# Stacked keys, split sums and fourteen moved pieces in a one-core transformer kernel

## The chip, the core and the metric

The kernel runs on one core of a Trainium2 chip. Its time is the device time of one execution in microseconds (us). The engines work at the same time and meet at semaphores: TensorE (PE; its weight loads are listed apart, as PEld), VectorE (DVE), ScalarE (ACT), GpSimd (POOL) and SyncE (SP), whose queue issues DMA transfers.

## The reference, cut to what matters

Six mixer layers and two feed-forward layers run over 512 tokens of width 1024: pooling, convolution, latent attention, pooling, and then two attention layers (l = 0, 1), each with a feed-forward layer. The attention layers compute eight heads of stick-breaking attention (dimension 64) and four of differential attention.

```python
z = jnp.einsum('bhqd,bhkd->bhqk', qblk, kh).astype(jnp.float32) * scale
strict = kpos[None, :] < qp[:, None]
log_beta = jax.nn.log_sigmoid(z)
log_keep = jnp.where(strict, jax.nn.log_sigmoid(-z), 0.0)
between = lax.cumsum(log_keep, axis=log_keep.ndim - 1, reverse=True) - log_keep
w = jnp.where(strict, jnp.exp(log_beta + between), 0.0)
```

Each layer begins with an RMS norm, `xf * rsqrt(mean(xf * xf) + eps) * g`, which needs the sum of squares over the 1024 features of each token.

## The kernel before

**Numbers.** Activations lie with features on the 128 partitions and tokens along the row. A float32 matrix is held as two tiles of the type fp32r, a high part and what is left (low). A product is then three matmuls, high x high, high x low, low x high (`mm3`, lines 414 to 416). ScalarE makes the high part (`high`, L941), VectorE the low part (`low`, L1556). Weights come by DMA into four `raw` tiles, 512 KB each; ScalarE copies them to `wh` (L932), VectorE (L1548) or GpSimd (L2327) makes `wl`. A weight unit of 128 columns in eight blocks is `gemm8`: 24 matmuls of 512 columns.

**Order.** Every engine has a program of its own, written out by hand, in `pe_program`, `act_program`, `dve_program`, `pool_program` and `sp_program`; each instruction waits for the results that it names and runs in its place. In an attention layer the order is a list of calls in `second_layer(l)` of each program. PSUM has eight banks. Three are kept for the stick-breaking scores (`sb_banks`), the others are taken in the order of `LAYER_BANKS`; a bank is waited for until its reader has marked it free.

**Sums of squares.** ScalarE squares, GpSimd adds up into `ACC`, and `sum_squares` (L442) multiplies by a matrix of ones in full float32, which the profile shows as two records. A use is a norm: 0 to 3 are the first four layers, "kv" and "q" the latent norms, 4 and 6 open the attention layers, 5 and 7 the feed-forward layers, ("df", l, h) the differential heads. ScalarE's `root` (L963) and VectorE's `recip_root` (L1564) turn the sum into the factor `R`, which the results of the projections are multiplied by afterwards; so the projections run ahead of it, and `gemm8(norm=...)` puts the sum inside a projection. The convolution layer calls `sum_squares(1)` between its first two projections (`cc`, `ch`; `cb` and `cz` follow).

**Stick-breaking scores.** `proj("sq", p)` and `proj("sk", p)` make queries and keys of two heads, 64 partitions each. VectorE scales them, `plain` splits them. `sb_scores(h)` multiplies for each of four key blocks (`GR`: 256 + 128, 384 and 512 columns in three banks) 64 rows of keys with 64 rows of queries, and adds a mask with 128-row products of `identr` and `hidden` (L752). Then follow `soft` (softplus; ACT, DVE), `keep` (split), `sb_between` (running sums on TensorE, L766 and L767), `weights_of` (exponential and split) and `sb_pv` (product with the values). `df_scores(h, base)` (L787 to L792) works on 64-row products of both halves of the partitions, `df_turn` transposes (L544), `df_pv` and `df_squares` follow, and `wo(half, m, parts)` is the output projection. `rot` splits a rotated query or key of the differential heads after GpSimd has added its parts (L2350).

Of the kernel before, what the change touches and what calls it, by code (L numbers as in the profile page):

```python
# [15 lines left out]
S = 512  # L16
# [20 lines left out]
for _name, _n in (("pool_norm0", 8), ("pool_norm1", 8), ("pool_scale0", 16), ("pool_scale1", 16),  # L37
# [26 lines left out]
LAYER_BANKS = (  # L64
# [3 lines left out]
LAST_BANKS = (0, 6, 5, 1, 3, 7, 2, 4)  # L68
LAST_ROWS = (1, 0, 4, 2, 3, 5, 7, 6)

SEMS = ("xin0", "xin1", "xin2", "xin3", "xin4", "xin5", "xin6", "xin7", "consts", "vec", "raw0", "raw1", "raw2", "raw3", "pos", "lam", "cos", "sin", "fn", "out",
        "group", "whi", "wlo", "wlop", "act", "dve", "pool")
# [25 lines left out]
class Counts:  # L98
# [7 lines left out]
    def mark(self, name, *results, by=1):  # L106
        self.total[name] += by
        for r in results:
            assert r not in self.value or r[0] in ("accfree", "wfree", "stored"), r
            self.value[r] = (name, self.total[name])  # L110
        return self.sems[name], by
# [176 lines left out]
def program(nc, D, out):  # L288
    ctx = ExitStack()
    with ctx:  # L290
# [66 lines left out]
        def sqk(p):  # L357
            return (YH[2], YL[2], YH[3], YL[3]) if p == 1 else G[8:12]
# [22 lines left out]
        def linit(l):  # L381
            return 0.8 - 0.6 * math.exp(-0.3 * l)

# [8 lines left out]
        def pe_program(handle, c):  # L392
# [25 lines left out]
            def gemm8(key, h, l, ready=None, norm=None):  # L418
# [277 lines left out]
            def second_layer(l):  # L696
# [38 lines left out]
                def sb_scores(h):  # L735
                    p, e = h // 2, h % 2
                    q_h, q_l, k_h, k_l = sqk(p)
                    rr = slice(64 * e, 64 * e + 64)
                    pe.wait_ge(*at("pl", l, "sq", p))
                    pe.wait_ge(*at("pl", l, "sk", p))  # L740
                    pe.wait_ge(*at("ones"))
                    for n, (kbs, k0, width) in enumerate(GR):
                        b = use(sb_banks[n], ("ss", l, h, kbs[0]))
                        for kb in kbs:
                            o = b[:, KOFF[kb] - k0:KOFF[kb] - k0 + 512 - 128 * kb]
                            kc, qc = slice(kb * 128, kb * 128 + 128), slice(kb * 128, 512)
                            mm3(o, k_h[rr, kc], k_l[rr, kc], q_h[rr, qc], q_l[rr, qc], kb == kbs[0], False)
                    for kbs, k0, width in GR:
                        b = ps("ss", l, h, kbs[0])
                        for kb in kbs:  # L750
                            o = b[:, KOFF[kb] - k0:KOFF[kb] - k0 + 128]
                            mm = pe.do.matmul(o, identr[:, :], hidden[:, :], start=False, stop=kb == kbs[-1])  # L752
                        mm.then_inc(*mark("group", ("mm", "ss", l, h, kbs[0])))
# [71 lines left out]
                v_part(0, 0, 0), norms(), v_part(0, 0, 1), proj("sq", 0), proj("sk", 0), v_part(0, 1, 0)  # L825
                sb_scores(0), proj("dq", 0), v_part(0, 1, 1), proj("dk", 0)
                sb_between(0), proj("sq", 1), sb_scores(1), df_scores(0, 34), sb_pv(0), proj("dk", 1)
                proj("sk", 1)
                sb_between(1), df_scores(0, 32), df_scores(0, 16), proj("dk", 2), proj("dq", 1), sb_scores(2)
                v_part(1, 1, 0), df_turn(0), v_part(1, 1, 1), sb_pv(1), v_part(1, 0, 0), df_scores(1, 34)  # L830
                v_part(1, 0, 1)
                sb_between(2), sb_scores(3), df_pv(0), df_scores(1, 32), df_scores(1, 16), proj("dq", 2)
                df_squares(0), proj("dq", 3), sb_pv(2), proj("sk", 2), proj("sq", 2), df_scores(2, 34)
                df_turn(1)
                sb_between(3), df_pv(1), df_scores(2, 32), sb_scores(4), df_scores(2, 16), proj("dk", 3)
                df_squares(1), sb_pv(3), proj("sq", 3), df_turn(2)
                sb_between(4), df_pv(2), df_scores(3, 34), sb_scores(5), df_scores(3, 32), wo(0, 2), wo(0, 0)
                sb_pv(4), proj("sk", 3), df_scores(3, 16)
                sb_between(5), wo(0, 1), df_squares(2), sb_scores(6), wo(0, 4), df_turn(3), sb_pv(5), df_pv(3)
                wo(0, 5), wo(0, 3)  # L840
                sb_between(6), wo(0, 6), sb_scores(7), sb_pv(6), df_squares(3), wo(1, 2, (0, 1))
                wo(1, 1, (0, 1)), wo(0, 7), wo(1, 0, (0, 1))
                sb_between(7), wo(1, 1, (2,)), wo(1, 4, (0, 1, 2)), wo(1, 3, (0, 1, 2)), sb_pv(7)
                wo(1, 0, (2,)), wo(1, 2, (2,)), wo(1, 1, (3,)), wo(1, 0, (3,)), wo(1, 4, (3,)), wo(1, 2, (3,))
                wo(1, 3, (3,)), wo(1, 5), wo(1, 7), wo(1, 6)
# [67 lines left out]
        def act_program(handle, c):  # L913
# [312 lines left out]
            def second_layer(l, done):  # L1226
# [27 lines left out]
                def plain(nm, p):  # L1254
                    dst = sqk(p)[0 if nm == "sq" else 2]
                    if p > 1:
                        act.wait_ge(*at("mm", "ss", l, 2 * p - 3 if p == 2 else 5, 0))
                    high(dst[:, :], temp("pj", l, nm, p), ("pj", l, nm, p), ("plh", l, nm, p))
# [97 lines left out]
                soft(0)  # L1356
                keep(0)
# [6 lines left out]
                weights_of(0)  # L1364
                taking('sq', l, 1)
                rot("dk", 0)
                taking('dk', l, 1)
# [1368 lines left out]
```

## Time and profile before

| | |
|---|---|
| median of 3 runs | 2719.13 us (2718.26 to 2719.65) |
| the profiled execution | 2719.73 us |
| its span, first to last instruction | 2717.9 us |
| TensorE busy | 99% of the span |
| VectorE, ScalarE, GpSimd busy | 58%, 42%, 23% |
| TensorE's share of the chain that ended last | 93% |
| mean granted clock of TensorE | 0.998 |

Times in the rows are in us from the start of the span. A matmul's record runs from its start until its results have landed, and records overlap; how fast matmuls follow each other is read from start to start. `128x512` is partitions x columns. A view's brackets give the idle time of the engine before an instruction, and who ended it.

### The profile page before, as it was taken

How to read it: one execution, taken by the hardware profiler on the slowest of the kernel's cores; microseconds unless marked ns; L12 is line 12 of the kernel's file. 1: busy time of each engine (PE TensorE's matmuls, PEld its weight loads, DVE VectorE, ACT ScalarE, POOL GpSimd, SP SyncE). 2: the span in 40 equal slices, each digit the busy share in tenths (PEclk: the TensorE clock that was granted, in tenths of full speed). 3: DMA queues.
4: the chain of work that ended last, by engine and by line, in shares of the span. 5: the costliest groups of instructions: out<-in, count | busy, mean ns of one | idle time of the engine just before them, and what ended most of it. 6: DMA issues, size and time to landing. Idle time of an engine off the chain costs nothing.

```text
span 2717.9 us, 31965 instructions
## 1 busy us (share of the span) xinstructions
PE 2694.4 (99%) x12918; PEld 2254.4 (83%) x12918; DVE 1576.7 (58%) x2307; ACT 1150.4 (42%) x1831; POOL 625.6 (23%) x401
## 2 busy tenths in 40 slices
PE   8999999999999999999999999999999999999999
PEld 7888888888888888888888888788888888788887
DVE  7556545344466646665575678744445668754444
ACT  4323323222347636533235767422224667522223
POOL 1000111011136525400004642411102452411100
PEclk9999999999999999999999999999999999999999
DMA  4232332332221222222322221233333221233332
GB/s 162 95 99 93 99 100 93 101 101 93 90 80 56 72 69 67 93 95 99 96 98 88 80 68 33 85 94 101 93 101 102 72 63 47 70 97 97 94 99 79
DMA packets 69412, 238.78 MB, mean 88 GB/s; under 512 B 7696, under 2 KB 10256, under 8 KB 69264
## 3 DMA queue, kind: packets, MB, share of 16 engines
q1 hardware_dynamic: 69264, 236.73, 27.6%
q8 instruction: 102, 1.67, 0.3%
q14 instruction: 46, 0.38, 0.0%
HBM read 234.60 MB, written 2.10 MB: 87 GB/s over the span
## 4 chain that ended last, share of the span: by engine, by line
PE 93%; DVE 3%; ACT 2%; POOL 1%; issue 0%; DMA 0%; SPq 0%; ACTq 0%; POOLq 0%
PE ps L414 30%; PE ps L416 29%; PE ps L415 29%; DVE ptl L1556 1%; PE ps L544 1%; PE ps L442 1%; ACT wh L932 0%; PE ps L767 0%; PE ps L766 0%; POOL acc L2336 0%; PE ps L604 0%; PE ps L605 0%; ACT pth L941 0%; DMA raw<-in_pool_in 0%; PE ps L466 0%
## 5 line engine op out<-in xcount | busy, mean ns | idle before, releaser
L932 ACT ACTIVATE wh<-raw 128x1024 fp32r<-128x1024 f32 (+2 forms) x453 | 465.0, 1028 | 741.7 <-PE ps L416 738.5
L414 PE MATMUL ps<-xh,wh 128*128 128x512 f32 x1920 | 753.5, 392 | 0.0
L416 PE MATMUL ps<-xh,wl 128*128 128x512 f32 x1920 | 747.5, 389 | 0.0
L415 PE MATMUL ps<-xl,wh 128*128 128x512 f32 x1920 | 747.3, 389 | 0.0
L1548 DVE TENSOR_TENSOR wl<-raw,wh 128x1024 fp32r<-128x1024 f32 (+1 forms) x339 | 449.4, 1326 | 151.2 <-ACT wh L932 151.0
L414 PE MATMUL ps<-yh,wh 128*128 128x512 f32 x1088 | 425.1, 391 | 2.6 <-ACT t L960 1.6
L414 PEld LDWEIGHTS ps<-xh,wh 128*128 128x128 f32 x1920 | 360.5, 188 | 76.4 <-issue 2.2
L415 PEld LDWEIGHTS ps<-xl,wh 128*128 128x128 f32 x1920 | 360.5, 188 | 76.0 <-issue 2.2
L415 PE MATMUL ps<-yl,wh 128*128 128x512 f32 x1088 | 423.5, 389 | 0.0
L416 PE MATMUL ps<-yh,wl 128*128 128x512 f32 x1088 | 423.4, 389 | 0.0
L416 PEld LDWEIGHTS ps<-xh,wl 128*128 128x128 f32 x1920 | 360.3, 188 | 75.2
L2327 POOL TENSOR_TENSOR wl<-raw,wh 128x1024 fp32r<-128x1024 f32 (+2 forms) x114 | 255.4, 2249 | 378.1 <-ACT wh L932 378.0
L1582 DVE TENSOR_TENSOR x<-ps,x 128x512 f32<-128x512 f32 x152 | 104.3, 689 | 265.2 <-PE ps L416 265.2
L2336 POOL TENSOR_TENSOR acc<-acc,t 128x512 f32<-128x512 f32 x59 | 84.1, 1425 | 721.2 <-ACT t L953 719.2
L414 PEld LDWEIGHTS ps<-yh,wh 128*128 128x128 f32 x1088 | 204.2, 188 | 48.2 <-issue 4.3
L416 PEld LDWEIGHTS ps<-yh,wl 128*128 128x128 f32 x1088 | 204.2, 188 | 42.6
L415 PEld LDWEIGHTS ps<-yl,wh 128*128 128x128 f32 x1088 | 204.3, 188 | 41.7
L2521 POOL TENSOR_TENSOR t<-t 128x512 f32<-128x512 f32 x64 | 71.2, 1116 | 513.4 <-DVE t L2256 513.4
L941 ACT ACTIVATE yh<-t 128x512 fp32r<-128x512 f32 x148 | 93.1, 631 | 169.4 <-POOL t L2521 56.7
L1556 DVE TENSOR_TENSOR yl<-t,yh 128x512 fp32r<-128x512 f32 x148 | 114.6, 775 | 82.7 <-ACT yh L941 82.7
L1560 DVE SCALAR_TENSOR_TENSOR xl<-x,vec,xh 128x512 fp32r<-128x512 f32 x64 | 83.1, 1315 | 60.3 <-ACT xh L943 60.3
L2256 DVE SCALAR_TENSOR_TENSOR t<-ps,r 128x512 f32<-128x512 f32 x64 | 44.1, 689 | 104.3 <-PE ps L416 104.0
(261 smaller groups left out, 3647.7 us busy)
## 6 DMA issues: line engine op xcount, KB each, us to landing
raw<-in_ff SPq DMA_DIRECT2D x120, 512.0 KB, 3.6
raw<-in_pool_in SPq DMA_DIRECT2D x64, 512.0 KB, 3.3
raw<-in_conv_in SPq DMA_DIRECT2D x64, 512.0 KB, 3.3
raw<-in_pool_out SPq DMA_DIRECT2D x32, 512.0 KB, 3.3
raw<-in_qk SPq DMA_DIRECT2D x32, 512.0 KB, 3.7
raw<-in_pool_grp SPq DMA_DIRECT2D x16, 512.0 KB, 3.3
raw<-in_conv_out SPq DMA_DIRECT2D x16, 512.0 KB, 3.3
raw<-in_mla_z SPq DMA_DIRECT2D x16, 512.0 KB, 3.6
```

The source lines that it names most:

```text
L414: pe.do.matmul(o, lh, rh_, start=start, stop=False)
L415: pe.do.matmul(o, lh, rl_, start=False, stop=False)
L416: return pe.do.matmul(o, ll, rh_, start=False, stop=stop)
L932: act.do.activation(h[:, 0:ncol], r[:, 0:ncol], ACT.Copy).then_inc(*mark("whi", ("whi", k)))
L941: act.do.activation(dst, src, ACT.Copy).then_inc(*mark("act", done))
L1548: dve.do.tensor_tensor(lo[:, 0:ncol], r[:, 0:ncol], f(h[:, 0:ncol]), ALU.subtract).then_inc(*mark("wlo", ("wlo", k)))
L1556: dve.do.tensor_tensor(dst, src, f(h), ALU.subtract).then_inc(*mark("dve", *done))
L1560: dve.do.scalar_tensor_tensor(dst, src, scale, f(h), ALU.mult, ALU.subtract).then_inc(*mark("dve", *done))
L1582: dve.do.tensor_tensor(x[m][:, :], ps(*key)[:, :], x[m][:, :], ALU.add).then_inc(*mark("dve", ("psfree",) + key, *done))
L2327: pool.do.tensor_tensor(lo[:, 0:ncol], r[:, 0:ncol], f(h[:, 0:ncol]), ALU.subtract).then_inc(*mark("wlop", ("wlo", k)))
L2336: pool.do.tensor_tensor(ACC[:, :], ACC[:, :], temp("sq", use, k), ALU.add).then_inc(*mark("pool", ("acc", use, k), ("tfree", "sq", use, k)))
L2521: pool.do.tensor_tensor(t, t, t, ALU.mult).then_inc(*mark("pool", ("ffs",) + key))
```

## The change

Stacked keys: a key tile of a pair of heads becomes two tiles. Tile e holds the high part of head e's keys on that head's partitions, and the low part on the other 64. The high part of the query is put on both halves of the partitions by DMA copies inside the chip, issued by ScalarE (two for the even head, one, `double`, for the odd). One 128-row matmul then gives high x high and low x high, a 64-row matmul the third product. The mask of the two joined blocks is one matmul. Split sums: for uses 1, 2, 3, 5 and 7 `ACC` is split into high and low, and the sum is two fp32r matmuls; the place of the sum inside the projection changes for all uses that `gemm8` places. The rest are moves within the programs; new bank lists go with them.

```diff
-LAYER_BANKS = (
+LAYER_BANKS = (
...
+SUMS_SPLIT = (1, 2, 3, 5, 7)
+NORM_AT = 5
...
         def sqk(p):
-            return (YH[2], YL[2], YH[3], YL[3]) if p == 1 else G[8:12]
+            q0, ql_, k0, k1 = (YH[2], YL[2], YH[3], YL[3]) if p == 1 else G[8:12]
+            return (q0, (YL[1], YH[1], YH[2], YH[3])[p]), ql_, (k0, k1)
...
+        def sum_parts(use):
+            return (PTH[:, 0:S], PTL[:, 0:S]) if use == 2 else (DFH[:, 0:S], DFL[:, 0:S])
...
-                    if norm is not None and k == 2:
+                    if norm is not None and k == (NORM_AT if norm in SUMS_SPLIT else 4):
                         sum_squares(norm)
...
+                if use in SUMS_SPLIT:
+                    pe.wait_ge(*at("ones"))
+                    pe.wait_ge(*at("suml", use))
+                    h, lo = sum_parts(use)
+                    pe.do.matmul(b[:, :], onesr[:, :], h, start=True, stop=False)
+                    pe.do.matmul(b[:, :], onesr[:, :], lo, start=False, stop=True).then_inc(
+                        *mark("group", ("mm", "rs", use)))
+                    return
...
-                              norm=st if g == 0 and i == (1 if j else 3) else None)
+                              norm=st if g == 0 and i == 3 else None)
...
                         xgemm(1, "cc", i, first=i == 0)
-                        if i == 0:
-                            sum_squares(1)
-                        xgemm(1, "ch", i)
+                        xgemm(1, "ch", i, norm=1 if i == 0 else None)
...
-                    pe.wait_ge(*at("pl", l, "sk", p))
+                    pe.wait_ge(*at("plx", l, p) if e == 0 else at("pl", l, "sk", p))
+                    pe.wait_ge(*at("dup", l, p, e))
...
-                            mm3(o, k_h[rr, kc], k_l[rr, kc], q_h[rr, qc], q_l[rr, qc], kb == kbs[0], False)
+                            pe.do.matmul(o, ks[e][:, kc], qs[e][:, qc], start=kb == kbs[0], stop=False)
+                            pe.do.matmul(o, ks[e][rr, kc], q_l[rr, qc], start=False, stop=False)
...
+                        o, cover = b[:, 0:128], hidden[:, :]
+                        if len(kbs) == 2:
+                            o = b[:, 0:512].rearrange("p (a c) -> p a c", a=2)[:, :, 0:128]
+                            cover = hidden[:, :].rearrange("p (a c) -> p a c", a=1).to_broadcast([128, 2, 128])
+                        pe.do.matmul(o, identr[:, :], cover, start=False, stop=True).then_inc(
+                            *mark("group", ("mm", "ss", l, h, kbs[0])))
...
 def root (ACT):
+                if use in SUMS_SPLIT:
+                    high(sum_parts(use)[0], ACC[:, :], last_square(use), ("sumh", use))
...
 def recip_root (DVE):
+                if use in SUMS_SPLIT:
+                    h, lo = sum_parts(use)
+                    low(lo, ACC[:, :], h, ("sumh", use), ("suml", use), ("accfree", use))
...
 def plain (ACT):
+                    if nm == "sk":
+                        high(ks[0][0:64, :], t[0:64, :], ("pj", l, nm, p), ("plhx", l, p))
+                        high(ks[1][64:128, :], t[64:128, :], ("pj", l, nm, p), ("plh", l, nm, p))
+                        return
...
+                    high(qs[1][:, :], t, ("pj", l, nm, p), ("plh", l, nm, p))
+                    act.wait_ge(*at("plh", l, nm, p))
+                    for rr in (slice(0, 64), slice(64, 128)):
+                        act.do.dma_start(f(qs[0][rr, :]), f(qs[1][0:64, :])).then_inc(*mark("dupa", ("dup", l, p, 0), by=16))
+
+                def double(p):
+                    q = sqk(p)[0][1]
+                    act.wait_ge(*at("dup", l, p, 0))
+                    act.wait_ge(*at("pl", l, "sq", p))
+                    if l or p:
+                        act.wait_ge(*at("dup", l, p - 1, 1) if p else at("dup", l - 1, 3, 1))
+                    act.do.dma_start(f(q[0:64, :]), f(q[64:128, :])).then_inc(*mark("dupb", ("dup", l, p, 1), by=16))
...
 def plain (DVE):
+                    if nm == "sk":
+                        low(ks[0][64:128, :], t[0:64, :], ks[0][0:64, :], ("plhx", l, k), ("plx", l, k))
+                        low(ks[1][0:64, :], t[64:128, :], ks[1][64:128, :], ("plh", l, nm, k), ("pl", l, nm, k),
```

`double(0)` and `double(1)` stand on ScalarE behind `soft(0)` and `keep(1)`, `double(2)` and `double(3)` behind `df_exp(2, 34)` and `df_exp(3, 16)`.

The moves, per engine. TensorE: `df_scores(0, 32)` ahead of `sb_between(1)`; `sb_scores(3)` from before `df_pv(0)` to behind `df_scores(1, 16)`; `df_scores(3, 32)` from behind `sb_scores(5)` to before `df_scores(3, 34)`; `df_turn(3)` ahead of `wo(0, 4)`; `wo(1, 3)` ahead of `wo(1, 4)`. ScalarE: `weights_of(0)` from before `taking("sq", 1)` to behind `rot("dk", 0)`; `x_high(st + 1, 1)` behind `x_high(st + 1, 2)`. VectorE: `df_join(0)` and `turned("dk", 2)` behind `rot("dk", 1)` and `turned("dq", 1)`; `v_low(1, 0)` ahead of `between(2)`; `df_max(2, 34)` ahead of `df_turn(1)`; `sb_out(3)` ahead of `between(4)`. GpSimd: the first two value units change places, and `scale_x(7)` with `taking("v", 0, 1, 1)` comes before `scale_x(5)`.

## Rows read from the trace of the kernel before

**Rows 1.** The page: its span and the busy time of each engine.

```profile
span 2717.9 us, 31965 instructions
...
PE 2694.4 (99%) x12918; PEld 2254.4 (83%) x12918; DVE 1576.7 (58%) x2307; ACT 1150.4 (42%) x1831; POOL 625.6 (23%) x401
...
```

**Rows 2.** Timeline, TensorE, head 0: start us, duration us, engine, line, operation.

```profile
...
1495.09 0.28 PE L416 MATMUL ps<-wh,xl 128*128 128x256 f32 x1
...
1495.52 0.28 PE L415 MATMUL ps<-g 64*128 64x256 f32 x1
1495.64 0.28 PE L416 MATMUL ps<-g 64*128 64x256 f32 x1
...
1496.27 0.33 PE L415 MATMUL ps<-g 64*128 64x384 f32 x1
1496.44 0.33 PE L416 MATMUL ps<-g 64*128 64x384 f32 x1
...
1496.85 0.39 PE L415 MATMUL ps<-g 64*128 64x512 f32 x1
1497.08 0.39 PE L416 MATMUL ps<-g 64*128 64x512 f32 x1
...
```

**Rows 3.** Timeline, TensorE's weight loads, the same head.

```profile
...
1495.30 0.18 PEld L414 LDWEIGHTS ps<-g 64*128 64x128 f32 x1
...
1497.40 0.52 PEld L752 LDWEIGHTS ps<-hidden,identr 128*128 128x128 f32 x4 [0.37 <-issue]
1497.84 0.19 PEld L414 LDWEIGHTS ps<-xh,wh 128*128 128x128 f32 x1
...
```

**Rows 4.** Waits of TensorE, first attention layer: total us, times, longest us.

```profile
...
PE ps L414 <- ACT t L960: 0.8, 1, 0.8
...
```

**Rows 5.** DMA issues: KB each, median us from issue to landing.

```profile
...
t<-in_lam SPq DMA_DIRECT2D x2, 128.0 KB, 2.0
...
```

**Rows 6.** Timeline, TensorE, the sum of squares of use 1.

```profile
...
322.00 1.02 PE L442 MATMUL ps<-acc,const 128*128 128x512 f32 x2
...
323.09 0.40 PE L415 MATMUL ps<-xl,wh 128*128 128x512 f32 x1
...
```

**Rows 7.** Timeline, TensorE, the sum of squares of use 0.

```profile
...
27.48 0.39 PE L416 MATMUL ps<-xh,wl 128*128 128x512 f32 x1
28.59 1.12 PE L442 MATMUL ps<-acc,const 128*128 128x512 f32 x2 [0.72 <-POOL acc L2336]
...
```

**Rows 8.** Timeline, VectorE and TensorE, start of the convolution layer.

```profile
...
325.11 3.35 DVE L1564 RECIPROCAL r<-t 128x512 f32<-128x512 f32 x1 [3.94 <-ACT t L963]
...
329.90 1.22 DVE L1548 TENSOR_TENSOR wl<-raw,wh 128x1024 fp32r<-128x1024 f32 x1
...
333.78 0.39 PE L414 MATMUL ps<-xh,wh 128*128 128x512 f32 x1
...
```

**Rows 9.** Timeline, all engines, around the first differential scores.

```profile
...
1517.59 0.53 ACT L1297 ACTIVATE s<-s 128x384 f32<-128x384 f32 x1 [0.33 <-PE ps L767]
...
1518.96 1.53 POOL L2350 TENSOR_TENSOR t<-t 128x512 f32<-128x512 f32 x1 [0.32 <-DVE t L1716]
...
1520.20 0.63 ACT L941 ACTIVATE pth<-s 128x512 fp32r<-128x512 f32 x1
...
1522.33 2.47 DVE L1556 TENSOR_TENSOR yl<-t,yh 128x512 fp32r<-128x512 f32 x1 [0.78 <-ACT yh L941]
...
1525.70 0.50 PE L787 MATMUL ps<-yh 64*128 64x512 f32 x1
...
```

**Rows 10.** Busy time by stretch; PEclk is the mean granted clock.

```profile
...
1690.00:1710.00 20.00, 18.84 (x89) 15.31 (x88) 13.22 (x21) 11.37 (x21) 5.08 (x2) 0.91 0.18 53
1702.00:1704.00 2.00, 2.00 (x7) 1.81 (x7) 1.97 (x5) 0.00 (x0) 0.00 (x0) 0.50 0.46 172
2323.00:2326.00 3.00, 3.00 (x12) 2.71 (x11) 2.55 (x6) 0.00 (x0) 0.00 (x0) 0.50 0.39 137
...
```

**Rows 11.** Timeline, TensorE, the product behind the scores of head 7.

```profile
...
1701.35 0.65 PE L414 MATMUL ps<-pth,g 128*128 128x512 f32 x1 [0.38 <-DVE ptl L1556]
...
```

More of the change, by code:

```diff
@@ L108, in mark @@
         for r in results:
-            assert r not in self.value or r[0] in ("accfree", "wfree", "stored"), r
+            assert r not in self.value or r[0] in ("accfree", "wfree", "stored", "dup"), r
             self.value[r] = (name, self.total[name])
@@ L845, in second_layer @@
-                wo(1, 3, (3,)), wo(1, 5), wo(1, 7), wo(1, 6)
+                v_part(0, 0, 0)
+                norms()
+                v_part(0, 0, 1)
+                proj("sq", 0)
+                proj("sk", 0)
+                v_part(0, 1, 0)
+                sb_scores(0)
+                proj("dq", 0)
+                v_part(0, 1, 1)
+                proj("dk", 0)
+                sb_between(0)
+                proj("sq", 1)
+                sb_scores(1)
+                df_scores(0, 34)
+                sb_pv(0)
@@ new lines, in second_layer @@
+                proj("dk", 1)
+                proj("sk", 1)
+                df_scores(0, 32)
+                sb_between(1)
+                df_scores(0, 16)
+                proj("dk", 2)
+                proj("dq", 1)
+                sb_scores(2)
+                v_part(1, 1, 0)
+                df_turn(0)
+                v_part(1, 1, 1)
+                sb_pv(1)
+                v_part(1, 0, 0)
+                df_scores(1, 34)
+                v_part(1, 0, 1)
+                sb_between(2)
@@ new lines, in second_layer @@
+                df_pv(0)
+                df_scores(1, 32)
+                df_scores(1, 16)
+                sb_scores(3)
+                proj("dq", 2)
+                df_squares(0)
+                proj("dq", 3)
+                sb_pv(2)
+                proj("sk", 2)
+                proj("sq", 2)
+                df_scores(2, 34)
+                df_turn(1)
+                sb_between(3)
+                df_pv(1)
+                df_scores(2, 32)
+                sb_scores(4)
+                df_scores(2, 16)
@@ new lines, in second_layer @@
+                proj("dk", 3)
+                df_squares(1)
+                sb_pv(3)
+                proj("sq", 3)
+                df_turn(2)
+                sb_between(4)
+                df_pv(2)
+                df_scores(3, 32)
+                df_scores(3, 34)
+                sb_scores(5)
+                wo(0, 2)
+                wo(0, 0)
+                sb_pv(4)
+                proj("sk", 3)
+                df_scores(3, 16)
+                sb_between(5)
+                wo(0, 1)
@@ new lines, in second_layer @@
+                df_squares(2)
+                sb_scores(6)
+                df_turn(3)
+                wo(0, 4)
+                sb_pv(5)
+                df_pv(3)
+                wo(0, 5)
+                wo(0, 3)
+                sb_between(6)
+                wo(0, 6)
+                sb_scores(7)
+                sb_pv(6)
+                df_squares(3)
+                wo(1, 2, (0, 1))
+                wo(1, 1, (0, 1))
+                wo(0, 7)
+                wo(1, 0, (0, 1))
+                sb_between(7)
@@ L846, in second_layer @@
+                wo(1, 1, (2,))
+                wo(1, 3, (0, 1, 2))
+                wo(1, 4, (0, 1, 2))
+                sb_pv(7)
+                wo(1, 0, (2,))
+                wo(1, 2, (2,))
+                wo(1, 1, (3,))
+                wo(1, 0, (3,))
+                wo(1, 4, (3,))
+                wo(1, 2, (3,))
+                wo(1, 3, (3,))
+                wo(1, 5)
+                wo(1, 7)
+                wo(1, 6)
                 first_pair(st + 1, [("f1", l, 0, 0), ("f1", l, 0, 1)], LAST_ROWS)
@@ L1464, in second_layer @@
                 taking('wo', l, 1, 1)
-                x_high(st + 1, 1)
                 x_high(st + 1, 0)
@@ L1469, in second_layer @@
                 x_high(st + 1, 2)
+                x_high(st + 1, 1)
                 taking('wo', l, 1, 3)
@@ L2467, in second_layer @@
                 taking('v', l, 0, 1, 0)
+                scale_x(7)
+                taking('v', l, 0, 1, 1)
                 scale_x(5)
```

62 lines of the change are left out of this document (24 added, 38 removed), and 3 rows, old and new, of the table LAYER_BANKS.

## The prediction

> **What bounds the kernel now.** I read the page first: TensorE is busy 2694.4 of 2717.9 us, so in this kernel only TensorE's own instructions and its waits can move the time; the other engines matter where TensorE waits for them [rows 1]. A busy share says little about how fast an instruction gives way to the next, so the second view was TensorE's timeline around one head of the stick-breaking scores, read by the distance from start to start. Three-pass products of 128 rows follow each other every 0.12 us with 256 columns; in the scores, 384 columns take 0.17 (1496.27 to 1496.44) and 512 take 0.23 (1496.85 to 1497.08) [rows 2]. The weight loads beside them show what the matmul rows hide. Four loads in a row, from 1497.40 to 1497.84, are 0.11 us each, so a 128-column product cannot go faster than 0.11. And where the number of active rows changes (128 to 64 at the start of the head, 64 to 128 at its end), the load does not run under the product before it: that product, started at 1495.09, has streamed by 1495.21, and the load starts at 1495.30; the one started at 1497.08 has streamed by 1497.31, and the load starts at 1497.40 [rows 2, 3]. Idle 0.09 plus a bare load of 0.11: a change of row count costs about 0.20 us. By the starts of the products it is 0.19 (1495.09 to 1495.52 is 0.43, for two products of 0.12). Third view: who TensorE waits for. In the first attention layer it has seven lines, the longest single wait 0.8 [rows 4]. So a layer is bound by TensorE, and the vector and scalar engines are just behind it in a few places.
>
> **Part 1, stacked keys.** Per head the score product of each of four key blocks goes from three matmuls to two: one of 128 rows (high and low keys stacked over a doubled query), one of 64 rows (high keys, low query). Saved: one each of 256, 128, 384 and 512 columns, 0.12 + 0.11 + 0.17 + 0.23 = 0.63 us [rows 2, 3]. The mask goes from four products of 128 columns to one of 256 and two of 128: 0.44 becomes 0.34, so 0.10 more. But the two kinds now alternate. Before, a head is one run of 64-row products: two changes. Now it is 128, 64, 128, 64, 128, 64, 128, 64 and then the mask (128): eight changes, four runs. Two of the products between changes have 128 columns and need only their 0.06 of streaming (128 columns of the 0.23 for 512), since the load is already in the price of the change: 2 x 0.05 = 0.10 comes off. Savings per head 0.83, for 8 heads and 2 layers 13.3 us.
>
> Runs of 64-row products in a layer, counted along TensorE's program. Before: the eight heads and ten pieces of differential scores, of which two touch a head's run (df 2/32 with head 4, df 3/34 with head 5): 16 runs. After: 8 x 4 = 32 of the heads, and ten of the differential scores (0/32 and 0/16 are torn apart by `sb_between(1)`, 3/32 and 3/34 are joined), none of which can merge, because a head now begins with a 128-row product: 42 runs. That is 26 more runs, 52 more changes a layer, 104 in all, at 0.195: +20.3 us (19.8 to 20.8 by the two readings). **Part 1: 20.3 - 13.3 = +7.0 us.** A head by itself goes from 2.74 us (1495.21 to 1497.95, which is the last load's start plus 0.11) to about 3.08.
>
> The rule for this is in the Trainium skill. "TensorE: Matmul & The Clock Gate", section "Step-by-step: what each phase is for", says that TensorE pulls a weight load ahead of a running matmul when it goes to the background buffer; by that alone the changes would be free and part 1 would be -11.7 us. The loads at 1495.30 and 1497.40 were not pulled ahead [rows 3], so I keep it as a rival only.
>
> **Part 2, what part 1 asks of the others.** Each key tile is split in halves: one more scalar-engine copy and one more vector subtraction per pair. TensorE waits for the first half alone for the even head, so nothing is later for it. The doubled query comes by copies of 128 KB, three per pair, issued by the scalar engine. A load of that size lands 2.0 us after its issue [rows 5]; between the query's projection and the first scores lie a projection (24 x 0.227 = 5.4 us) and a value part (48 x 0.12 = 5.8 us), and for the other pairs more. I count the copies at nothing; uncovered, a copy would cost at most its 2.0 us per pair, 16 us in all, at the least nothing. The same window hides the halves. The issue itself holds the scalar engine; no row shows a copy inside the chip or an issue there, so between 0 and 2.0 us each, near 0 since the engine only hands it over.
>
> **Part 3, split sums.** A sum of squares in full precision takes, from 322.00 to 323.09 less the 0.23 of the product that stands between, 0.86 us [rows 6]. Two single-pass products of 512 columns take 0.45. Five uses: 5 x -0.41 = **-2.0 us**. Use 0 stays as it is but is asked for six products (1.4 us) later. It is due at 27.48 + 0.23 = 27.71 and starts at 28.59, with a bare load of 0.11 [rows 7]: the accumulation is late by 0.9. Two more k-steps cover that: **-1.0**.
>
> Each moved sum makes its root later. In the convolution layer the sum moves from behind the first projection to k = 5 of the second: 15 x 0.227 = 3.4 later, less 0.4 for its two shorter products: 3.0. Behind it hang a table load, the root, the reciprocal of 3.35 us (325.11), and the low part of the fourth projection's weights, which ends at 329.90 + 1.22 = 331.12; TensorE starts that projection at 333.78 [rows 8]. Slack 2.7. After: ready 334.1, wanted 333.78 - 0.41 = 333.37, and a bare load on top: **+0.9 us**. At the other four (3.0 less six products) the root is 1.6 to 2.3 later, and TensorE has two or more projections of 5.4 us before it wants anything from it: nothing.
>
> **Part 4, the pieces that move.** `weights_of(0)` goes behind `rot("dk", 0)` on the scalar engine. That rotation needs the GpSimd sum which ends at 1518.96 + 1.53 = 1520.49. Now the weights' six activations start at 1517.59 and end at 1520.83; after the move they start at 1521.1 and end at 1524.4. The vector engine takes the low parts first and the rotation's after them: 1525.1 plus 0.7 to 2.5 (it took 2.47 at 1522.33, beside GpSimd): 1525.8 to 1527.6. The differential scores 0/34, at 1525.70 now and 0.35 later by head 1, want it at 1526.05 [rows 9]. So 0 to 1.5 us a layer; I take 0.7: **+1.4**. Queued behind it on the scalar engine are `plain("sq", 1)` and the softplus of head 1, for which `sb_between(1)` has 10 us. The mirror of it: two waits are covered by longer heads, the one in front of `sb_pv(6)` (0.35 of its 0.38 [rows 11]) and the first output projection (0.3): 0.65 a layer, **-1.3**. The sum-of-squares wait of 0.8 [rows 4] stays: the same bank is reused right behind it. The waits around 1647 to 1651 hang on the vector engine after head 4 and move along with it. The swaps among the output projections, `x_high(1)`, `scale_x(7)` and the two value units on GpSimd lie more than a projection ahead of their readers: nothing, at worst one subtraction (0.7) each way.
>
> **Part 5, the clock.** The granted clock is 0.50 (1.2 GHz) at 1702 to 1704 and at 2323 to 2326 [rows 10]; before the first, TensorE did the scores of head 7 and waited 0.38 [rows 11]. A mean of 0.91 over 20 us is 0.09 x 20 / 0.5 = 3.6 us at 0.50, of which half, 1.8, is lost each time. The new scores hold more idle time per head than the old. From two such falls to all sixteen heads is 14 x 1.8 = +25, to none -3.6; I take one more, as heads 4 and 6 now stand beside other thin work: **+1.8**. On this "TensorE: Matmul & The Clock Gate" (section "A second HAM failure mode: psum-queue depth-cycling") says that frequent short idles between groups of matmuls make the clock swing; the trace shows it at two places of sixteen.
>
> **Sum.** +7.0 - 2.0 - 1.0 + 0.9 + 1.4 - 1.3 + 1.8 = +6.8 us on the profiled execution's 2719.73, of which 1.8 lie outside its span. The median of the runs shown is 0.6 below it. Forecast 2719.13 + 6.8 = **2725.9 us**, slower by 0.25%. This kernel's runs differ by 0.05%; 0.2% (5.4 us) is what a measurement can tell from no change.
>
> **Rivals.** *A: the changes of row count are free*, since weights load ahead; the place is each head, and it decides as soon as a change costs under 0.13 us (13.3 / 104). Part 1 becomes -11.7; the sum is then -11.7 - 2.0 - 1.0 + 0.9 + 1.4 = -12.4, of which the vector engine's chain gives back 1 or 2 at the waits around 1647: 2708, faster. For it: different rows of the array could be loaded independently. Against it: all the changes in the trace cost 0.19 or more. *B: the clock stays up.* The longer head 7 covers the wait before `sb_pv(6)`, the two falls vanish, and `rot` is in time: 7.0 - 3.0 + 0.9 - 1.3 - 3.6 = 0.0, 2719.1, no change. For it: that wait, of 0.38, stands right before the fall. Against it: the idle time inside the heads grows. *C: the clock falls at most light heads*, say five more times: +9.0 in place of +1.8, 2733. For it: two heads of sixteen do it already.
>
> **Chances.** Forecast 0.45 (its own range 2721 to 2730), A 0.10, B 0.28, C 0.17. Range 2716 to 2735: it leaves out A and the far end of C. Faster by over 0.2% is A: 0.10. Within 0.2%: B and the lower quarter of the forecast, 0.37. Slower: the rest and C, 0.53.
>
> **What would show it.** In the changed profile, weight loads of the scores that start 0.09 after the end of streaming at every change, a head of 3.1 us; sums of 0.45; a wait of 0.9 on the fourth projection's weights near 333; no wait near 28; a wait of up to 1.5 before the first differential scores; granted clock 0.50 in two to four places. Wrong it is if a head takes under 2.7 us (then A), if the differential scores wait for nothing, or if a wait for a copy of the queries appears.

## The result and the profile after

| | before | changed |
|---|---|---|
| median | 2718.26 us (13 runs, 2716.45 to 2719.65) | 2726.14 us (13 runs, 2723.34 to 2738.17) |
| profiled execution | 2719.73 | 2738.17 |
| its time at granted clock 0.50 inside the layers | 6.8 us | 34.1 us |
| the same execution without what that cost (half of it) | 2716.3 | 2721.1 |

The ratio is 1.0037, interval 1.0030 to 1.0044: slower by 7.9 us, forecast 6.8. The profiled execution is one of three of the thirteen in which the clock was low for longer, so the two profiles are compared without the clock: +4.8 us (forecast without its clock term: +5.0). That leaves some 3.1 of the 7.9 to the clock in the median run, and less if the subtraction takes off too much (see the experiments). One execution of the kernel before, of 27 that ran beside e4, e6, e7 and e8, took 13369.91 us and is left out of the ratios.

The page of the changed kernel, against [rows 1]:

```profile
span 2736.4 us, 31864 instructions
...
PE 2708.6 (99%) x12838; PEld 2256.4 (82%) x12838; DVE 1585.1 (58%) x2320; ACT 1158.6 (42%) x1844; POOL 619.8 (23%) x401
```

TensorE issues 80 products fewer and is busy 14 us longer. Timeline of TensorE, head 0, against [rows 2]:

```profile
1493.51 0.28 PE L757 MATMUL ps<-g 128*128 128x256 f32 x1
1493.72 0.38 PE L758 MATMUL ps<-g 64*128 64x256 f32 x1
...
1495.28 0.50 PE L757 MATMUL ps<-g 128*128 128x512 f32 x1
1495.71 0.50 PE L758 MATMUL ps<-g 64*128 64x512 f32 x1
1496.14 0.56 PE L765 MATMUL ps<-hidden,identr 128*128 128x256 f32 x3
1496.54 0.45 PE L417 MATMUL ps<-xh,wh 128*128 128x512 f32 x1
```

Its weight loads, against [rows 3]:

```profile
1494.91 0.18 PEld L758 LDWEIGHTS ps<-g 64*128 64x128 f32 x1 [0.19 <-issue]
1495.28 0.19 PEld L757 LDWEIGHTS ps<-g 128*128 128x128 f32 x1 [0.19 <-issue]
1495.71 0.18 PEld L758 LDWEIGHTS ps<-g 64*128 64x128 f32 x1 [0.25 <-issue]
```

Two products of 512 columns are 0.43 apart, not 0.23: at a change of row count each load begins with the product's own record, 0.09 after the one before has streamed, and none is ahead. This head is 3.03 us (1493.51 to 1496.54). Waits of TensorE in the first layer (total, times, longest), against [rows 4]:

```profile
PE ps L800 <- DVE yl L1669: 2.1, 1, 2.1
PE ps L417 <- DVE ptl L1669: 1.9, 2, 1.6
PE ps L553 <- DVE t L2102: 0.8, 1, 0.8
PE ps L417 <- ACT t L1051: 0.8, 1, 0.8
PE ps L779 <- DVE ptl L1669: 0.5, 1, 0.5
```

6.1 us, where before it was 4.0 in seven lines. The wait before `sb_pv(6)` and the one before the first output projections are gone as forecast. New are the 2.1 (before `df_scores(3, 32)`), the 1.6 of the second line (before the value product `df_pv(1)`) and the 0.8 before the transposes of `df_turn(1)`. The granted clock in stretches of the first layer, against [rows 10]:

```profile
1525.00:1528.00 3.00, 3.00 (x11) 1.98 (x8) 2.68 (x5) 1.80 (x5) 1.25 (x1) 0.50 0.50 109
...
1658.00:1668.00 10.00, 9.86 (x28) 6.56 (x29) 7.09 (x17) 6.38 (x14) 0.00 (x0) 0.50 0.13 51
```

A third, of 3.4 us, begins at 1634.05, and the same three places show it in the second layer. Before them stand head 1, head 4, and, at 1658, the new wait of 2.1.

### The profile page after: what moved, and what is told of

It reads as the page before. It is cut to its first block, busy times and chain, and to the rows that moved or that the text cites. A ratio compares the mean times of both kernels' runs of the same rounds, so it can differ in the third digit from the quotient of the medians.

```text
span 2736.4 us, 31864 instructions
## 1 busy us (share of the span) xinstructions
PE 2708.6 (99%) x12838; PEld 2256.4 (82%) x12838; DVE 1585.1 (58%) x2320; ACT 1158.6 (42%) x1844; POOL 619.8 (23%) x401
## 4 chain that ended last, share of the span: by engine, by line
PE 93%; DVE 4%; ACT 2%; issue 1%; ACTq 0%; DMA 0%; SPq 0%; DVEq 0%
PE ps L417 29%; PE ps L419 29%; PE ps L418 29%; DVE ptl L1669 1%; PE ps L758 1%; PE ps L553 1%; PE ps L757 1%; PE ps L779 1%; PE ps L780 1%; DVE yl L1669 1%; PE ps L486 0%; PE ps L613 0%; PE ps L614 0%; ACT t L1157 0%; PE ps L453 0%
## 5 line engine op out<-in xcount | busy, mean ns | idle before, releaser
L1030 ACT ACTIVATE yh<-t 128x512 fp32r<-128x512 f32 (+1 forms) x152 | 95.7, 631 | 181.0 <-POOL t L2641 58.5
```

The costliest lines, as they stand in the source:

```text
L1030: act.do.activation(dst, src, ACT.Copy).then_inc(*mark("act", done))
```

## The experiments

"Against before" is the difference of medians to runs of the kernel before on the same chip (medians 2717.64 to 2718.26). "Clock-free" is the profiled execution less half its time at 0.50. It is an estimate from one execution, and can be off by 2 us or more. The start of the kernel alone moves it: the changed kernel and the seven that differ from it only in the attention layers have the same program up to the convolution's sum of squares, and begin that sum between 324.32 us (e2) and 325.82 (e7). And it takes off too much where TensorE would have waited anyway. Of each execution that was timed without a profile the record has the mean granted clock to three digits, where 0.001 is 2.7 us. In e8 those at 1.000 took 2716.9 to 2717.5 us and one at 0.997 took 2717.65, though half of its time at 0.50 is 6.8 us or more; the column says 2714.9 for e8. Of the changed kernel one took 2726.63 at 0.999 and another 2725.28 at 0.997: without half of their time at 0.50 they are at least 4 us apart. Differences between kernels below are of these two columns.

| kernel | median | against before | ratio, interval | clock-free |
|---|---|---|---|---|
| before | 2718.26 | | | 2716.3 |
| changed | 2726.14 | +7.9 | 1.0037 (1.0030 to 1.0044) | 2721.1 |
| e1 scores grouped | 2714.82 | -2.9 | 0.9991 (0.9982 to 1.0000) | 2713.5 |
| e2 all score products 128 rows | 2713.39 | -4.3 | 0.9984 (0.9975 to 0.9993) | 2713.0 |
| e3 before, masks in between | 2744.00 | +26.3 | 1.0096 (1.0082 to 1.0109) | 2723.6 |
| e4 before, split sums | 2715.37 | -2.3 | 0.9992 (0.9983 to 1.0002) | 2713.3 |
| e5 changed, not stacked | 2719.32 | +1.6 | 1.0008 (0.9999 to 1.0017) | 2712.5 |
| e6 changed, two waits on GpSimd | 2722.54 | +4.9 | 1.0019 (1.0010 to 1.0028) | 2714.5 |
| e7 grouped, two waits | 2708.75 | -8.9 | 0.9966 (0.9953 to 0.9979) | 2709.1 |
| e8 grouped, no moves | 2719.15 | +1.5 | 1.0003 (0.9994 to 1.0012) | 2714.9 |
| e9 grouped, three waits | 2706.97 | -10.9 | 0.9960 (0.9947 to 0.9972) | 2706.7 |
| e10 as e9, one move undone | 2707.18 | -10.7 | 0.9956 (0.9943 to 0.9970) | 2707.4 |

**e3: changes of row count alone.**

```diff
 in the loop over key blocks:
     mm3(o, k_h[rr, kc], k_l[rr, kc], q_h[rr, qc], q_l[rr, qc], kb == kbs[0], False)
+    o = b[:, KOFF[kb] - k0:KOFF[kb] - k0 + 128]
+    mm = pe.do.matmul(o, identr[:, :], hidden[:, :], start=False, stop=kb == kbs[-1])
 (and not in a loop behind it)
```

> The kernel before, with one edit: each mask product (128 rows) stands right behind the three 64-row products of its block and not behind all twelve. Nothing is added or taken away. Changes of row count per head go from 2 to 8, 96 more in all. Theory: 96 x 0.195 = +18.7, less 0.05 for each of three masks per head whose load is in the price of the change (-2.4): +16.3, so 2718.3 becomes 2734.6, and a head grows from 2.6 to 3.6 us. Rival A (changes are free): 2718. A price half as large, if a part is hidden by the next product's streaming: 2726.

Timeline of TensorE, head 2 of e3:

```profile
1559.78 0.38 PE L414 MATMUL ps<-yh 64*128 64x256 f32 x1
...
1560.12 0.27 PE L416 MATMUL ps<-yh,yl 64*128 64x256 f32 x1
1560.33 0.33 PE L749 MATMUL ps<-hidden,identr 128*128 128x128 f32 x1
1560.58 0.32 PE L414 MATMUL ps<-yh 64*128 64x128 f32 x1
...
1563.35 0.50 PE L414 MATMUL ps<-wh,xh 128*128 128x256 f32 x1
```

The head is 3.57 us (1559.78 to 1563.35) against 2.60 for the same sixteen products in the old order: 0.97 for six changes and 0.15 saved, 0.19 a change. Rival A is out. The median rose by 26.3, more than the 16.3 expected, and the clock is why: nine stretches at half clock, 44.4 us, of which this is one (columns as in [rows 10]).

```profile
1598.00:1604.00 6.00, 6.00 (x25) 4.94 (x24) 0.78 (x2) 1.32 (x4) 0.00 (x0) 0.50 0.22 81
```

Clock-free it is +7.3, where sixteen heads have 15.5 more: in the first layer waits fall from 4.0 to 2.3 us, so some 3.4 of it is cover for waits; the other 4.8 no view accounts for, and part of it is what the subtraction takes off too much in nine stretches. Alternating row counts alone brings the clock down here: the edit only reorders, and TensorE's waits are shorter than before.

**e5: the changed kernel without the stacked keys.**

```diff
-pe.do.matmul(o, ks[e][:, kc], qs[e][:, qc], start=kb == kbs[0], stop=False)
-pe.do.matmul(o, ks[e][rr, kc], q_l[rr, qc], start=False, stop=False)
+mm3(o, k_h[rr, kc], k_l[rr, kc], q_h[rr, qc], q_l[rr, qc], kb == kbs[0], False)
 (key tiles, masks and splits as before; no copies)
```

> The changed kernel without the stacked keys: products, masks, key tiles and the absence of copies are those of the kernel before; split sums and all moves stay. The forecast's sum for these is -2.0 - 1.0 + 0.9 + 1.4 - 1.3 = -2.0, or 0 without the cover that the longer heads give: 2716 to 2718, 8 to 10 us under the changed kernel. Rival (the stacked keys cost nothing, the moves do): 2723 to 2726. The profile tells which of the new waits (2.1 before a differential score, 1.6 before a value product) belong to the moves: they stay here if they do.

The stacked keys cost 6.3 us in the median (forecast part 1: 7.0), clock-free 8.6. Waits of its first layer:

```profile
PE ps L795 <- DVE yl L1642: 2.2, 1, 2.2
PE ps L416 <- DVE ptl L1642: 1.3, 2, 0.9
```

The wait of 2.2 is there without the stacked keys; the split sums alone (e4) have 1.3 before the differential scores that stand at that point, the kernel before 0.4, so the moves bring the rest. All waits of this layer are 4.8 us, 1.3 less than in the changed kernel, whose waits before `df_pv(1)` and `df_turn(1)` are longer. The median is above the 2716 to 2718 expected, the clock-free time below them.

**e4: the kernel before with the split sums alone** (the sum's hunks of the diff, no others).

> The kernel before with the split sums alone: uses 1, 2, 3, 5 and 7 as two single-pass products behind five k-steps, use 0 behind four, the convolution's inside its second projection. No stacked keys, no moves. The forecast's terms: -2.0 - 1.0 + 0.9 = -2.1. The trace of the changed kernel shows no wait where the +0.9 was expected (the weights' low part ends at 332.28, the projection starts at 332.85), which would make it -3.0: 2714.7 beside a before of 2717.7. Rival: the sums were hidden by the vector engine's chain in the layers and only the front gains: -2.2. Rival: nothing, 2717.7.

-2.3 in the median, an interval that just reaches no change, and -3.0 clock-free. The executions at a mean clock of 1.000 are clearer: three of e4 took 2714.2 to 2715.3 us, seven of the kernel before, run beside it, 2716.3 to 2717.2. With e5 that gives the moves, without stacked keys: clock-free -0.8, in the median +3.9. The loss is in the clock: the mean is 0.996 to 0.998 in all executions of e5, 0.998 to 1.000 in e4's.

**e1: the 64-row products of a head together.**

```diff
 for each of the four key blocks:
+    pe.do.matmul(o, ks[e][rr, kc], q_l[rr, qc], start=kb == kbs[0], stop=False)
 then for each of them again:
+    pe.do.matmul(o, ks[e][:, kc], qs[e][:, qc], start=False, stop=False)
```

> The changed kernel, with one edit: in each head of the stick-breaking scores the four 64-row products come first, then the four 128-row ones, then the masks. Same products, same columns; only the changes between 64 and 128 active rows are fewer. Counted along TensorE's program a layer has 42 runs of 64-row products now and 15 with the edit (three pieces of differential scores merge with a head): 54 changes fewer a layer, 108 in all. Theory (each change costs 0.195 us): -21.1, and +1.6 for 128-column products that are bound by their load again, so about -19.5: 2726.1 becomes 2706.6, and a head takes 2.7 us in place of 3.03 to 3.12... less in the profile by 0.3 or more; below 2704 if the clock falls less often. Rival A (the changes are free): 2726, same. Rival B (the loss is the vector engine's waits, and faster heads only make them longer): 2715 to 2722, waits of TensorE grow by 4 to 6 us a layer.

Timeline of TensorE, head 0 of e1:

```profile
1493.94 0.90 PE L757 MATMUL ps<-g 64*128 64x256 f32 x4
1494.77 0.90 PE L763 MATMUL ps<-g 128*128 128x256 f32 x4
1495.51 0.46 PE L770 MATMUL ps<-hidden,identr 128*128 128x256 f32 x3
1495.80 0.45 PE L417 MATMUL ps<-xh,wh 128*128 128x512 f32 x1
```

The head falls from 3.03 to 1.86 with 0.09 more ahead of it: 1.08 less, by the price 6 x 0.195 - 0.10 = 1.07 (the head of 2.7 in the expectation was a slip). But of 19.5 us only 10.8 arrive. Clock-free e1 is no faster than e5, which does not stack at all (2713.5 and 2712.5, closer than that column can tell apart). Some of its waits in the first layer, 10.2 us in all (6.1 in the changed kernel, 4.8 in e5):

```profile
PE ps L417 <- ACT ob L1445: 2.3, 2, 1.3
PE ps L417 <- DVE ptl L1674: 2.2, 2, 1.6
PE ps L805 <- DVE yl L1674: 1.7, 2, 1.2
```

TensorE's products in a layer take 5.8 us less than e5's by their distances (0.227, 0.173, 0.12, 0.11), and it waits 5.4 longer for the vector and scalar engines instead. What e1 gains on e5 is clock, by the same column: 6.8 us at 0.50 in place of 13.7, and 1.3 lost in the median run in place of 6.8.

**e2: no 64-row product in a head at all.**

```diff
-pe.do.matmul(o, ks[e][rr, kc], q_l[rr, qc], start=False, stop=False)
+pe.do.matmul(o, ks[e][:, kc], q_l[:, qc], start=False, stop=False)
```

> The changed kernel, with the third score product (high keys, low query) taken over all 128 rows: it multiplies the stacked keys by both heads' low queries, so the low part of the scores is another one than in the reference; only its time is read. No head has a change of row count any more. Left are ten runs of differential scores a layer: 32 runs fewer, 128 changes in all. Theory: 128 x 0.195 = -25.0, +1.6 for the 128-column products: -23.4, so 2702.7, and a head of 2.2 to 2.3 us (two products each of 256, 128, 384 and 512 columns, 1.29, and masks 0.34 and a bare load or so). Rival A: 2726. Rival B (waits grow): 2712 to 2720.

An undisturbed head is 1.57 us, less than the 2.2 expected (by that sum 1.29 + 0.34 without a bare load), and the profile has no stretch at half clock inside the layers. But the median is 2713.4, 1.4 under e1, and the waits of the first layer grow to 11.7 us: rival B. Past the grouping, shorter heads buy nearly nothing.

**e6: GpSimd's splits held back.** The new wait of 2.1 in the changed kernel, in its timeline (GpSimd, VectorE, TensorE):

```profile
1653.90 2.82 POOL L2447 TENSOR_TENSOR wl<-raw,wh 128x1024 fp32r<-128x1024 f32 x1 [2.75 <-ACT wh L1021]
...
1654.41 2.86 DVE L1669 TENSOR_TENSOR yl<-t,yh 128x512 fp32r<-128x512 f32 x1
...
1658.14 0.65 PE L800 MATMUL ps<-yh 64*128 64x384 f32 x1 [2.13 <-DVE yl L1669]
```

```diff
 def second_layer (POOL), behind turned("dk", 3):
+pool.wait_ge(*at("kpl", l, 4, 0))
 taking('sq', l, 3)
+pool.wait_ge(*at("t1split", l, "dk", 3))
 taking('sk', l, 3)
```

> The changed kernel with two waits added on GpSimd: its weight split behind turned(dk, 3) waits for the last low part of keep(4), the next one for the low part of rot(dk, 3). Nothing else. In the profile of the changed kernel these splits (1648.45, 2.70 us; 1653.90, 2.82 us) run beside low parts on the vector engine that take 2.87 and 2.86 us in place of 0.69, and TensorE then waits 2.1 us for the second. Theory (the two engines block each other, and this is the wait): the low parts take 0.7, the wait falls to 0.3 or less, -1.8 to -2.1 a layer, and the stretch of 10.2 us at half clock behind it goes as well in the executions that have it: 2719 to 2722. Rival A (the order of the vector engine makes the wait, not GpSimd): 2726, and the wait stays at 1.5 or more. Rival B (the held splits are late for their own projections): 2727 or more, a wait for low weights near 1670.

The same place in e6:

```profile
1652.76 0.68 DVE L1669 TENSOR_TENSOR yl<-t,yh 128x512 fp32r<-128x512 f32 x1
1653.48 0.69 DVE L1669 TENSOR_TENSOR yl<-ps,yh 64x512 fp32r<-64x512 f32 x1
...
1653.66 2.41 POOL L2447 TENSOR_TENSOR wl<-raw,wh 128x1024 fp32r<-128x1024 f32 x1 [3.25 <-ACT wh L1021]
```

The low part takes 0.68, the wait is gone, the held split delays nobody. The second row reads PSUM and one tile of SBUF, and is not slowed beside GpSimd. This is what the Trainium skill says in "SBUF — State Buffer", section "Who interferes with whom": a vector instruction with two inputs in SBUF and a GpSimd instruction that reads SBUF take one port in turns, for the whole instruction, and one with a single SBUF input does not contend; the trace agrees (0.68 against 2.86 for the same instruction). The waits of the first layer fall from 6.1 to 2.1 us. Clock-free e6 gains 6.6, in the median 3.0, just outside the 2719 to 2722. The gap between the two is not a worse clock in the median run: both kernels' median runs have a mean of 0.998, at which the clock takes at most some 5 us inside the layers, not the 8.0 between e6's two columns. The 6.6 is too large, and why so little of the waits arrives in the median stays open.

**e7: both, grouped and held back** (e1 with e6's edit).

> Grouped order of the score products, and the same two waits on GpSimd. The grouped kernel's waits in the first attention layer are 9.2 us by the profile (0.6 + 0.8 + 1.4 + 1.5 of them between 1646 and 1656, behind low parts of 2.86 us). Theory (GpSimd's splits make these): -2 to -3 a layer, so 2714.8 becomes 2709 to 2711. Rival (the vector and scalar engines' chain is as long without the collisions, it only shifts): 2713 to 2715.

2708.75, 8.9 us faster than before and a little beyond the expected 2709 to 2711 (whose 9.2 should read 10.2). The waits on GpSimd are worth 6.0 here, 3.0 in e6: beside GpSimd's splits around 1645 e1 takes 4.89 us for three low parts and 2.03 for the instruction `ob<-ob,small,t` behind them, e7 2.72 and 0.97, and the waits that hung on them shrink (the one before `df_scores(3, 32)`, 1.2 in e1, is gone). No stretch at half clock inside the layers.

**e8: the moves, in the grouped kernel.** The kernel before with e4's sums and e1's stacked scores, no moves.

> The kernel before with the split sums and the stacked keys in grouped order, and none of the fourteen moves (the bank list is that of before). Against the grouped kernel it shows what the moves are worth. By the profiles, moves and sums together are worth -3.8 us without the clock (2716.3 to 2712.5), sums about -3: the moves -0.8. So 2715.6. Rival (the moves fit the new lengths and are what the stacked keys need): 2718 or more, with waits of TensorE before sb_pv and the differential scores. Rival (the moves are a loss since they line up GpSimd's splits with the vector engine's low parts and bring the clock down): 2711 to 2713.

The moves are worth 4.4 us in the grouped kernel: the first rival. Clock-free the profiles say 1.4; the executions at a mean clock of 1.000 say 2.4 to 3.4 (three of e8 at 2716.9 to 2717.5, four of e1 at 2714.1 to 2714.4). So the moves pay beside short heads, and cost 3.9 in the median without stacked keys (e5 against e4). In the alternating kernel no run tests them.

**e9: a third wait on GpSimd.** Vector engine and GpSimd in e7:

```profile
1606.07 5.64 DVE L1674 TENSOR_TENSOR ptl<-s,pth 128x384 fp32r<-128x384 f32 x3
1611.64 2.88 DVE L1674 TENSOR_TENSOR yl<-t,yh 128x512 fp32r<-128x512 f32 x1
...
1608.46 5.52 POOL L2452 TENSOR_TENSOR wl<-raw,wh 128x1024 fp32r<-128x1024 f32 x2
```

```diff
 behind turned("dq", 3):
+pool.wait_ge(*at("t1split", l, "dq", 2))
 taking('sk', l, 2)
```

> Grouped order, the two waits on GpSimd, and a third: its two weight splits behind turned(dq, 3) wait for the low part of rot(dq, 2). In the profile of the kernel with two waits these splits (1608.46, 5.52 us for both) run beside three low parts of 5.64 us in all (1606.07) and one of 2.88 (1611.64); free they would take about 1.6 and 0.7. The vector engine is then 3 to 4 us earlier at project(sq, 2), for which TensorE waits 1.1 at the turn behind it (1616.6), and 1.6 for the value product after (1621.0). Theory: -1.1 to -2.5 a layer: 2708.8 becomes 2704 to 2706.5. Rival (the scalar engine's exponentials hold the value product, and only the turn gains): 2706.5 to 2707. Rival (the held splits are late): 2709 or more.

The vector engine in e9:

```profile
1605.38 3.45 DVE L1674 TENSOR_TENSOR ptl<-s,pth 128x384 fp32r<-128x384 f32 x3
...
1609.95 2.50 DVE L1674 TENSOR_TENSOR yl<-ob,yh 128x512 fp32r<-128x512 f32 x1
1612.49 3.48 DVE L1674 TENSOR_TENSOR g<-t,g 64x512 fp32r<-64x512 f32 x2
```

-2.0 us: 2706.97 lies in the range of the first rival (2706.5 to 2707), and the waits agree with it. The one at the turn falls from 1.1 to 0.5, the one of 1.6 before the value product stays. The splits now slow the next low parts (2.50 and 3.48, where e7 has 0.67 and 1.41). 2706.97 is 10.9 us under before (0.9960, 0.9947 to 0.9972), and beats both kernels.

**e10: `weights_of(0)` back in its old place, in e9.**

> The kernel with three waits on GpSimd and grouped scores, with one of the fourteen moves undone: weights_of(0) stands ahead of rot(dk, 0) on the scalar engine again. TensorE waits 0.4 us (0.6 beyond the product's own length) for that rotation's low part in front of the first differential scores in the grouped kernels; in the changed kernel it was ready 0.6 us before. Forecast's theory (the move makes the rotation wait behind six activations, 0 to 1.5 us): undoing it gains up to 0.4 a layer, 0.8. Rival (the rotation was moved ahead of the exponentials in time; undone, its low part falls beside GpSimd's split and takes 2.5 us): undoing it loses 1 to 2 a layer, 2 to 4 us.

No difference (+0.2, intervals overlap), and neither of the two expected outcomes. Vector engine and GpSimd in e10, around the first differential scores:

```profile
1521.04 2.47 DVE L1674 TENSOR_TENSOR yl<-t,yh 128x512 fp32r<-128x512 f32 x1 [0.74 <-ACT yh L1035]
...
1520.56 5.20 POOL L2452 TENSOR_TENSOR wl<-raw,wh 128x1024 fp32r<-128x1024 f32 x2 [1.28 <-ACT wh L1026]
```

The rotation's low part falls beside GpSimd's splits again and takes 2.47 in place of 0.68, as the rival says, but it ends at 1523.51, before the scores (1523.66): the wait of 0.4 that e9 has there goes, and nothing is lost. The profile of e10 has another wait, 29 us earlier, in front of head 0, for a copy of the queries:

```profile
PE ps L757 <- DMA g<-yl: 0.7, 1, 0.7
```

## Why the forecast was right

**Part 1, +7.0: measured +6.3 in the median, +8.6 clock-free.** An undisturbed head takes 3.03 to 3.12 us (forecast 3.08); from the start of the product ahead of it to the start of the one behind, heads 0 to 2 are 0.32 to 0.34 longer than before (forecast 0.34). The trace has 168 changes of row count where the old one has 64: the 104 that were counted. At heads 4 and 5 of a layer, which no longer merge with the differential scores ahead of them, two more changes come on top: head 4 takes 3.32 from the end of streaming ahead of it (1630.02 to 1633.34), where a merged head took 2.59 (1652.58 to 1655.17, head 5 of the kernel before), so 0.73. That gives an estimate of 6 x 0.33 + 2 x 0.73 = 3.4 a layer, 6.9 in all, for the products; the 1.3 a layer that the changed kernel waits longer than e5 come on top, and between 6.3 and 8.6 no run decides. e3 isolates the price, 0.19. Of the rule of the Trainium skill that was cited there the traces show this much: between equal row counts a load runs ahead (in the changed kernel at 1493.39, for the product at 1493.51), at a change it does not (1495.71 for both).

**Part 2, nothing: right, with little to spare.** TensorE waits for no copy in the changed kernel. Their issue was left between 0 and 2.0; the scalar engine's queue gives about 0.6 each, and the two copies in front of head 0 land after:

```profile
1487.33 1.15 ACTq L1359 DMA_DIRECT2D g<-yl  x2
...
DMA to landing us min/median/max: 2.4/3.8/5.2
```

The prediction put 2.0 on a copy [rows 5], and most do land after 2.2 to 2.5. The second of these two, issued at 1487.9, takes 5.2 and is there 0.5 before head 0 begins at 1493.51. In e10, with the same instructions ahead of it, it takes 6.2, and TensorE waits the 0.7 shown there. What makes it late is open.

**Part 3, -2.1: measured -2.3, clock-free -3.0 (e4).** Two products take 0.47 where two records took 0.86 [rows 6], and use 0 starts without a wait [rows 7]:

```profile
29.53 1.02 PE L453 MATMUL ps<-acc,const 128*128 128x512 f32 x2
...
324.88 0.39 PE L447 MATMUL ps<-pth,onesr 128*128 128x512 f32 x1
325.12 0.39 PE L448 MATMUL ps<-ptl,onesr 128*128 128x512 f32 x1
325.35 0.40 PE L417 MATMUL ps<-xh,wh 128*128 128x512 f32 x1
```

The step of this part that failed is the +0.9 on the convolution's fourth projection: "Behind it hang a table load". It doesn't any more. The kernel before loads the table after the sum (1.28 us at 323.10). In the changed kernel the scalar engine, the low weights and their reader are:

```profile
319.06 0.61 ACT L1030 ACTIVATE pth<-acc 128x512 fp32r<-128x512 f32 x1
319.69 1.28 ACT L1054 ACT_TABLE_LOAD   x1
325.55 0.69 ACT L1054 ACTIVATE t<-ps,const 128x512 f32<-128x512 f32 x1 [4.57 <-PE ps L448]
...
331.06 1.22 DVE L1661 TENSOR_TENSOR wl<-raw,wh 128x1024 fp32r<-128x1024 f32 x1
...
332.85 0.39 PE L417 MATMUL ps<-xh,wh 128*128 128x512 f32 x1
```

The new `high` of the sum comes early, the load goes right behind it, and both are over long before the sum. The root starts 1.16 later than before (325.55 against 324.39), not 3.0, the low weights end at 332.28, and the product that reads them (the one of [rows 8]) starts on time, 0.6 later.

**Part 4, +0.1: wrong in its parts.** No run measures it in the changed kernel. Its -1.3 needs the longer heads; for the moves alone it has +1.4, and e5 against e4 measures -0.8 clock-free and +3.9 in the median. The +1.4 for `rot("dk", 0)` did not come: its low part ended at 1524.02, 0.6 before the scores, which wait for nothing; the prediction itself had named that as a sign of being wrong. Of its two prices, 0.7 and 2.5 us, the small one applied, because GpSimd's split had ended at 1521.28; against [rows 9], where the low part took 2.47, the move had carried it out of the collision, and e10, which undoes the move, has the 2.47 again. The mirror image was missed: `df_scores(3, 32)` waits 2.1 for a low part that now falls beside a split. I priced the slowdown at one place and did not look where else the shift would bring the two engines together.

**Part 5, +1.8: at most about +3.1.** Where it came near, it was by luck and not by its counting: it counted one fall more, and the profiled execution shows six stretches for two, two of them long. By the clock-free column the median run lost 5.0 to the clock against 1.9; since that column takes off too much, the true difference is smaller by an amount that no run gives. Rival B named `sb_pv(6)`: that fall did vanish, others came. Rival C describes three executions of thirteen, 2733.7 to 2738.2. What decides where the clock falls stays open: grouping (e1, e2, e7) removes most stretches and alternation (e3) makes nine, which shows the cause in kind; but e6, with fewer waits, has no better clock (means of 0.996 to 0.998, where ten of the changed kernel's thirteen have 0.997 to 0.999), and no run explains that.

The sum of 6.8 against 7.9 is thus sound in its largest term, the price of a change of row count. The other terms missed by some 1 to 2 us each, partly against each other, so that the total came this close is in part luck.

## What to carry over

Count, along TensorE's program, how often the number of active rows changes, before counting matmuls saved: here a change costs as much as 430 columns of a product (0.19 of 0.227 for 512), and putting the 64-row products of a head together turned a loss of 7.9 us into a gain of 2.9. When TensorE's work gets shorter in a kernel where other engines are just behind it, look next at which vector instructions with both inputs in SBUF run beside GpSimd; holding back a GpSimd instruction that nobody waits for freed a wait of 2.1 us a layer in e6 and cost nothing there, while in e9 the held splits slowed the next low parts. Compare executions without their time at half clock as well as by medians, since a reordering can gain in the one and lose in the other; but half of that time is only the most that the clock can have cost.

## What the runs showed that was not expected

- Executions of the same kernel differ by whole falls of the clock. Of 27 of the kernel before beside e1, eight took 2716.4 to 2717.0 us, fourteen 2717.4 to 2718.5 and five 2719.7 to 2720.0, with mean granted clocks of 1.000, 0.999 and 0.998 (a few of the first at 0.999). The profiled one, 2719.73, has two stretches of 3.4 us at 0.50, 1.7 us lost in each.
- GpSimd loses as well: its split takes 2.82 us beside the vector engine's low part and 2.41 when held back.
- A mask product that reads its 128 columns twice for the two joined blocks costs no more than a plain one of 256: in head 2 of e2 it and the two of 128 take 0.29 us together (1553.06 to 1553.35; 0.12 + 0.06 + 0.11).
